# Computing the conditioning vectors of a decoder layer in couples: four column groups of TensorE, each with its own tile of outputs

## The reference

```
mod = (jax.nn.silu(c) @ w_ada + b_ada)[:, None, :]
shift_m, scale_m, gate_m, shift_f, scale_f, gate_f = jnp.split(mod, 6, axis=-1)
h = modulate(rms_norm(x, g_pre_mix), shift_m, scale_m)
... MIX(h): projection with w_in, pooling, dilated attention, merge, w_out ...
x = x + gate_m * rms_norm(mix, g_post_mix)
h = modulate(rms_norm(x, g_pre_ffn), shift_f, scale_f)
... FFN(h): w_up, depthwise convolution, GeGLU, w_down ...
x = x + gate_f * rms_norm(ffn, g_post_ffn)
```

## Time and profile before

| | |
|---|---|
| time, median of 3 runs | 1033.84 us (1033.68 to 1034.89) |
| span of the profiled execution, first to last instruction | 1030.3 us |
| TensorE (matmuls) busy | 98% of the span |
| TensorE weight loads busy | 94% |
| VectorE, ScalarE, GpSimd busy | 46%, 38%, 11% |
| mean granted TensorE clock | 0.996 of full |

### The profile page before, as it was taken

One profiled execution on the slowest core, in us unless ns is written; L12 is line 12 of the kernel. 1 busy time (PEld: TensorE's weight loads), 2 busy tenths in 40 slices (PEclk: granted clock), 3 DMA queues, 4 the chain that ended last, 5 costly groups with the idle time before them and its releaser, 6 DMA issues.

```text
span 1030.3 us, 20618 instructions
## 1 busy us (share of the span) xinstructions
PE 1010.5 (98%) x8733; PEld 973.6 (94%) x8733; DVE 472.8 (46%) x856; ACT 388.5 (38%) x633; POOL 112.8 (11%) x175
## 2 busy tenths in 40 slices
PE   7999999999999999999999998999999999999996
PEld 6899999999999999998989988999999999999996
DVE  6733324422433233325856447465656565532323
ACT  5334422433244224433113346445445444422232
POOL 1000300040004100334913000000000000000000
PEclk9999999999999999999999999999999999999998
DMA  9966476667665777539996682666666666566412
GB/s 325 304 223 205 151 250 236 236 195 251 238 242 178 240 251 263 173 93 354 374 310 192 226 257 66 199 208 230 216 225 221 224 223 198 192 211 198 122 47 83
DMA packets 226473, 222.32 MB, mean 216 GB/s; under 512 B 6301, under 2 KB 189981, under 8 KB 225597
## 3 DMA queue, kind: packets, MB, share of 16 engines
q1 hardware_dynamic: 226297, 220.85, 64.7%
q10 hardware_dynamic: 84, 0.15, 0.0%
HBM read 213.56 MB, written 96.03 MB: 300 GB/s over the span
## 4 chain that ended last, share of the span: by engine, by line
PE 90%; POOL 4%; DVE 2%; issue 1%; DMA 1%; ACT 1%; SPq 0%; ACTq 0%; DVEq 0%; POOLq 0%
PE acc L1501 74%; POOL cached L685 3%; PE acc L1592 2%; PE psT L1712 2%; PE psT L1725 1%; PE psS L1551 1%; PE psT L1739 1%; PE psS L1695 1%; PE acc L1607 1%; PE acc L1599 1%; POOL tha L692 1%; PE psT L1582 1%; DVE w_lo L993 1%; PE psS L1693 1%; PE psT L1623 1%
## 5 line engine op out<-in xcount | busy, mean ns | idle before, releaser
L1501 PE MATMUL acc<-act_hi,w_hi 128*128 128x260 f32 x1856 | 380.6, 286 | 1.4 <-DVE w_lo L993 0.8
L1501 PE MATMUL acc<-act_hi,w_lo 128*128 128x260 f32 x1856 | 373.7, 283 | 0.0
L1501 PE MATMUL acc<-act_lo,w_hi 128*128 128x260 f32 x1856 | 373.1, 283 | 0.0
L993 DVE TENSOR_TENSOR w_lo<-raw,w_hi 128x1024 fp32r<-128x1024 f32 (+1 forms) x148 | 185.1, 1252 | 324.4 <-ACT w_hi L711 324.0
L1501 PEld LDWEIGHTS acc<-act_hi,w_hi 128*128 128x128 f32 x1856 | 285.4, 188 | 10.1 <-issue 7.3
L1501 PEld LDWEIGHTS acc<-act_hi,w_lo 128*128 128x128 f32 x1856 | 285.8, 188 | 0.0
L1501 PEld LDWEIGHTS acc<-act_lo,w_hi 128*128 128x128 f32 x1856 | 285.5, 188 | 0.0
L711 ACT ACTIVATE w_hi<-raw 128x1024 fp32r<-128x1024 f32 (+1 forms) x148 | 154.7, 1047 | 138.9 <-PE acc L1501 130.0
L1501 PE MATMUL acc<-g_hi,w_hi 128*128 128x260 f32 x352 | 71.6, 285 | 0.0
L1501 PE MATMUL acc<-g_hi,w_lo 128*128 128x260 f32 x352 | 70.8, 282 | 0.0
L1501 PE MATMUL acc<-g_lo,w_hi 128*128 128x260 f32 x352 | 70.7, 282 | 0.0
(11 more groups left out here) (284 smaller groups left out, 1002.4 us busy)
## 6 DMA issues: line engine op xcount, KB each, us to landing
out_k_sample<-in_cache_k_w SPq DMA_DIRECT2D x89, 368.0 KB
out_v_sample<-in_cache_v_w SPq DMA_DIRECT2D x89, 368.0 KB
raw<-in_w_in SPq DMA_DIRECT2D x60, 512.0 KB, 9.2
raw<-in_w_up SPq DMA_DIRECT2D x44, 512.0 KB, 5.5
ada_last<-in_w_ada SPq DMA_DIRECT2D x12, 1024.0 KB, 9.5
ada_first<-in_w_ada SPq DMA_DIRECT2D x9, 1024.0 KB, 9.7
raw<-in_w_down SPq DMA_DIRECT2D x16, 512.0 KB, 4.3
out_k_sample<-in_cache_k_w SPq DMA_DIRECT2D x16, 511.0 KB
```

The lines of the kernel that those rows point to most:

```text
L993: dve.tensor_tensor(w_lo[PLACE[n]][:, 0:cols], raw[:, n % RAW, 0:cols], w_hi[PLACE[n]][:, 0:cols].bitcast(F32), ALU.subtract).then_inc(lo_ ...
L1501: ins_ = pe.matmul(acc[b][:, half, 0:HALF], w, x[:, t, half * HALF:(half + 1) * HALF], start=first and i == 0 and j == 0, stop=last and i ...
```

## The change

The 24 blocks become 12 couples of four output tiles (512 columns). ADA now lists couples as pairs (lo, hi) of the first tiles of two adjacent ones. A block s is now one half of a couple's contraction tiles: even s holds contraction tiles 0 to 3, odd s tiles 4 to 7, for all four output tiles. Every column group j owns output tile j of the couple and sums all eight contraction tiles. So ada(s) issues 16 matmuls of 128 x 128 in place of eight of 128 x 256. The sums of a couple are 128 x 128 in place of two times 128 x 256; one transpose (one load, one matmul) turns them, in place of four folding matmuls (eight loads, eight matmuls). The evacuation copies 128 columns per couple, one modulation serves a couple. The first eight loads are two DMAs of 512 KB each, with rows of 1 KB; later loads stay one DMA of 1024 KB, with rows of 2 KB. In the pairs stage the two blocks of a couple run one after the other in passes 1 and 3, with one fold each there; passes 0 and 2 have none. fold4 is gone.

```diff
-ADA = [0, 4, 1, 5, 2, 6, 3, 7] + list(range(8, 24))
+ADA = [(2 * j, 8 + 2 * j) for j in range(4)] + [(4 * c, 4 * c + 2) for c in range(4, 12)]
...
-                sp.dma_start(ada_slot(s)[:, :, :], block_of(w_ada, ADA[s] * 2 * P, 2 * P)).then_inc(ada_in[s % 8], 16)
+                lo, hi = ADA[s // 2]
+                src = tiles(w_ada)[:, s % 2 * 4:s % 2 * 4 + 4, :]
+                if s < SADA:
+                    for x, t in enumerate((lo, hi)):
+                        sp.dma_start(ada_slot(s)[:, :, 2 * P * x:2 * P * x + 2 * P], src[:, :, t * P:(t + 2) * P]).then_inc(ada_in[s % 8], 16)
+                else:
+                    sp.dma_start(ada_slot(s)[:, :, :], src[:, :, lo * P:(lo + 4) * P]).then_inc(ada_in[s % 8], 16)
...
-                act.wait_ge(folded, OADA + 2 * c)
-                act.activation(ada_rows[:, :, :, :].rearrange("p s a b -> p (s a b)"), psA_late[c], ACT.Copy).then_inc(ada_rowed, 2)
+                act.wait_ge(folded, MIDDLE + c - 1)
+                act.activation(ada_rows[:, c % 4, :], sums_of(MIDDLE + c), ACT.Copy).then_inc(ada_rowed, 1)
...
-                for k in range(KT):
-                    ins_ = pe.matmul(out[32 * (k % 4):32 * (k % 4) + 32, :], siluT[:, MC * k:MC * k + 32], ada_slot(s)[:, k, :], start=k < 4, stop=k >= 4)
+                for i in range(KT // 2):
+                    k = s % 2 * 4 + i
+                    for j in range(4):
+                        ins_ = pe.matmul(sums_of(c)[32 * j:32 * j + 32, :], siluT[:, MC * k:MC * k + 32], ada_slot(s)[:, i, j * P:(j + 1) * P],
+                                         start=k == 0, stop=k == KT - 1)
...
-                for i in range(2):
-                    ins_ = pe.matmul(out[:, i * MC:(i + 1) * MC], ada_rows[:, s % 2, i, :], fold4[:, :], start=True, stop=True)
-                ins_.then_inc(folded, 1)
+                pe.transpose(psM_first[c % 2] if c < FIRST else psM, ada_rows[:, c % 4, :], ident[:, :]).then_inc(folded, 1)
...
-                    elif what == "ada":
-                        ada(SADA + p * NA + k)
+                    elif what == "ada" and p % 2:
+                        ada(SADA + p - 1)
+                        ada(SADA + p)
...
-                for i in range(4):
-                    ins_ = pe.matmul(psM_late[c][:, i * MC:(i + 1) * MC], ada_rows[:, i // 2, i % 2, :], fold4[:, :], start=True, stop=True)
-                ins_.then_inc(folded, 2)
+                pe.transpose(psM_late[c], ada_rows[:, c % 4, :], ident[:, :]).then_inc(folded, 1)
```

More of the change, by code:

```diff
@@ L999, in of, with ada_evac, modulation @@
                 return accv[SUM[s] % 2]
[L1001 to L1011, removed]
+            def ada_evac(c):
+                dve.wait_ge(ada_done, 2 * c + 2)
+                if c >= 2:
+                    dve.wait_ge(folded, c - 1)
+                dve.tensor_copy(ada_rows[:, c % 4, :], sums_of(c)).then_inc(ada_rowed, 1)
+            def modulation(c):
+                dve.wait_ge(folded, c + 1)
+                lo, hi = ADA[c]
+                dst = mod[:, lo:lo + 2 * (hi - lo), :].rearrange("p (a b) m -> p a b m", a=2)[:, :, 0:2, :]
+                dve.tensor_tensor(dst, turned_of(c), four_tiles(vec, c).unsqueeze(3).to_broadcast([P, 2, 2, MC]), ALU.add).then_inc(ada_out, 1)
             def gains(dst, k0, nk, scale0, g0, plus):
@@ L1088, in _ @@
             dve.wait_ge(vec_out, 1)
-            for s in range(2):
-                ada_evac(s)
+            ada_evac(0)
             dve.wait_ge(rs_ready, 1)
@@ L1098, in _ @@
                 c = slice(2 * j, 2 * j + 2)
-                for s in (2 * j, 2 * j + 1):
-                    modulation(s)
-                dve.wait_ge(ada_out, 2 * j + 2)
+                modulation(j)
+                dve.wait_ge(ada_out, j + 1)
                 gains(a_m, 2 * j, 2, 8, 48, 1.0).then_inc(gained, 1)
@@ L1217, in _ @@
                         take_values(p, k)
-                    elif what == "ada":
-                        ada_evac(SADA + p * NA + k)
-                    elif what == "fold" and (p or k >= 0):
-                        modulation(SADA + p * NA + k)
+                    elif what == "ada" and p % 2:
+                        ada_evac(FIRST + p // 2)
+                    elif what == "fold" and p % 2:
+                        modulation(FIRST + p // 2)
                     elif what == "stat" and p:
@@ L1374, in _ @@
                 if m == 7:
-                    late_modulation(1)
+                    modulation(MIDDLE + 1)
                 take_samples(("out", m), m, gg_m)
@@ L1387, in _ @@
                     split(N["up", 0, 1])
-                    late_modulation(0)
+                    modulation(MIDDLE + 0)
             inverse_root(2)
@@ L1400, in _ @@
             dve.tensor_reduce(sSum[:, :], sSq[:, :, :].rearrange("p k b -> p b k"), AX_X, ALU.add).then_inc(xs_new_summed, 1)
-            late_modulation(2)
+            modulation(MIDDLE + 2)
             inverse_root(3)
@@ L1412, in _ @@
                 scaled(t, 0, 2)
-            late_modulation(3)
-            dve.wait_ge(ada_out, OADA + 8)
+            modulation(MIDDLE + 3)
+            dve.wait_ge(ada_out, MIDDLE + 4)
             gains(a_f, 0, KT, 32, 64, 1.0).then_inc(gained, 1)
@@ L1641, in _ @@
             fold(0)
-            fold(1)
             busy(30)
@@ L1658, in _ @@
                 first_units(2 * j - 2)
-                fold(2 * j)
-                fold(2 * j + 1)
+                fold(j)
                 first_units(2 * j - 1)
@@ L1793, in _ @@
                         values(p, k)
-                    elif what == "ada":
-                        ada(SADA + p * NA + k)
-                    elif what == "fold" and (p or k >= 0):
-                        fold(SADA + p * NA + k)
+                    elif what == "ada" and p % 2:
+                        ada(SADA + p - 1)
+                        ada(SADA + p)
+                    elif what == "fold" and p % 2:
+                        fold(FIRST + p // 2)
                     elif what == "stat" and p:
@@ L1912, in late_ada @@
             def late_ada(s):
-                c, at = (s - OADA) // 2, s % 2 * 2 * P
-                if c == 0:
+                c = (s - OADA) // 2
+                if s % 2 == 0 and c == 0:
                     pe.wait_ge(conv_used, 2)
-                if 2 <= c < LATE - 1:
-                    pe.wait_ge(ada_rowed, OADA + 2 * c - 2)
-                if c == LATE - 1:
+                if s % 2 == 0 and 2 <= c < LATE - 1:
+                    pe.wait_ge(ada_rowed, MIDDLE + c - 1)
+                if s % 2 == 0 and c == LATE - 1:
                     pe.wait_ge(rows_out, 8)
[L1921 to L1925, removed]
+                ada(s)
             def late_couple(c):
```

90 lines of the change are left out of this document (43 added, 47 removed).

## The result

The changed kernel takes 1025.97 us (median of 4 runs, 1025.8 to 1026.3), the kernel before 1034.37 beside it (1033.68 to 1034.93): ratio 0.9923, 95% interval 0.9909 to 0.9937. The nearest case was the rival to which I gave 0.2, that the feed doesn't bind (1026.9).

What follows compares the result with a forecast made beforehand. It took TensorE, busy 98% of the span, to bound the kernel. Terms -1.3 - 1.0 - 2.8 + 1.0 + 1.9 = -2.2 us, rounded to -2.1, took the median 1033.84 to 1031.8 us; range 1026.6 to 1037.5.

Steps and rivals of the forecast that it cites:

- the feed doesn't bind: Rival: 31 ns belongs to small turnings, not the sequencer, so bursts cost little more; -6.9, 1026.9 us, chance 0.2.
- the feed: On TensorE: the sequencer hands over an instruction every 31 ns, so two blocks in a row take 2.19 us against 1.86.
- a lead of instructions lying ready: Ahead of TensorE: instructions handed over early, at least 24 by one row, taken as 64, which shortens a burst's wait.
- Start stretch: Start of the kernel: cheaper folds and smaller copies against short leads and longer couples; net -1.2, with shorter modulation -1.3 us.
- the loads: Rival for the start: if split first loads land 1.3 us later, the start gains nothing; 1033.1 us, chance 0.1.
- Pairs stage: Pairs stage on TensorE: folds -1.4 us net of turnings, four single blocks becoming two bursts +0.4; net -1.0 us.
- Late folds: Late stage: folds 0, 1, 4 and 5 each become one turning of 0.11 us; together -2.8 us.
- Couples 0, 1 and 5: Late stage: three bursts of two blocks each take 0.33 us longer; together +1.0 us.
- Second norm: Second norm: doubled instructions end at 622.8 us, delaying the matmul that sums the samples and VectorE's norm; +1.9 us.
- the streaming rival: Rival that the columns streamed, not the handing over of instructions, set a burst; sum -6.9, 1026.9 us, chance 0.2.
- SyncE's wait for block 10: Fourth pass: SyncE waits some 6 us, hidden with 4 to spare; as a rival starving a unit, 1036 us, chance 0.05.
- What would show it: Test in the pairs stage: a burst of 2.1 to 2.3 us confirms feed and lead, 1.9 nothing binds, over 2.6 short lead.

Runs made afterwards that it cites:

- tiny_b: Changed kernel with 30 filler turnings ahead of block 2 replaced by three series with little to stream; one run, 1034.57 us, of no use as a time.
- two_loads: Changed kernel without the loads of blocks 2 to 7, which read two loaded slots again (output differs); 1025.48 us, ratio 0.9911.
- whole_loads: Changed kernel with its first eight loads whole (1 MB each) and both blocks of a couple run once both are there; 1028.04 us, ratio 0.9932.
- c0_after: The changed kernel again, no edit, as control beside the kernel before; 1025.96 us, ratio 0.9912.
- fold8: Changed kernel with each of the twelve folds issued as eight equal turnings; 1033.22 us, ratio 0.9993.
- c0_before: The kernel before again, unchanged, for a second profiled execution; 1034.79 us, ratio 1.0005.
- before_fill_b: The kernel before with useless filler turnings in the gaps of its second norm; 1032.74 us, ratio 0.9988.
- last_in_norm: Changed kernel with the last couple (blocks 22 and 23) moved from the up stage into gaps of the second norm; 1023.52 us, ratio 0.9893.
- halves: Changed kernel with every matmul of w_ada issued as two over 64 columns each; 1032.28 us, ratio 0.9976.
- group_order: Changed kernel with the 16 matmuls of a block issued one column group after another; 1050.02 us, ratio 1.0148.

## Why the prediction was wrong

The step that failed is **the feed**: "I read it as the rate at which TensorE's sequencer hands them over". The rate came from eight turnings with 128 weight columns, and I took for the instruction's price what was its weight load's. tiny_b varied that width (and the output's height with it) and the price fell from 64 to 27 ns a pair, the latter even at half the clock. And the burst that it was to price, 64 matmuls with their loads, took 1.88 us in place of the forecast's 2.19. The Trainium skill (TensorE: Matmul & The Clock Gate, section "LDWEIGHTS (loading the stationary operand)") says that a load's time follows the number of weight columns, not of rows. By that rule the row was a load's row, and the trace agrees (64 against 27 ns). I had cited the same page for about 62 ns per matmul, where firmware decodes them; here 64 matmuls of w_ada with their loads take 1.88 us, 29 ns each, and those of tiny_b's third series 15, so that price doesn't bind in this kernel. It looked confirmed because two different causes give nearly the same number.

My own row spoke against it: four blocks at 26 ns an instruction. I saved the theory with a lead of instructions lying ready, and then priced that lead at 64. The lead carried three of the four positive terms.

By the terms of the sum:

1. *Start stretch*, -1.3 forecast, -0.6 seen. The size was off for a reason that I had as a rival: the loads. The last landed at 38.50 (29.97 + 8.53) where before it was 36.5. By streaming the start was to gain 2.3; two_loads gains 2.5 (0.6 + 1.95). I had blamed the splitting; whole_loads shows that it is at most a small part. Of the 2 us between 0.7 and 1.7 stand already in the issue of the second group of first loads (14.86 us, and 14.29 in c0_after, against 13.15 and 13.61 in the two profiles of before). With whole loads it is 14.37, so the splitting doesn't make that part either; its cause stays open. TensorE's faster work then has nothing to run on. The 0.15 to 0.3 us that the forecast gave each of blocks 0, 1 and 3 for a short lead don't follow from its own rule, which gives 0.36 to 0.54 for leads of 27 and 21; no run shows such a term at all.
2. *Pairs stage*, -1.0 forecast, -2.5 seen. The bursts were to cost +0.4 and gave -0.5: a couple adds 0.9 us to a block's place and takes away a whole other block with its entry and exit, 1.15 by the starts of the units behind it. The folds gave -2.0, not -1.4: those that are left cost less on the chain than I took, since entering them is shorter too. No cover, as I had said.
3. *Late folds* -2.8, seen -2.7 (4 x 0.68 on the chain): right, and the largest single part; fold8 takes it back. *Couples 0, 1 and 5* +1.0, seen +0.06 (3 x 0.02).
4. *Second norm* +1.9, seen -0.25. The doubled instructions were done in time; L1973 waits for VectorE. The 10.35 us of supply for 334 instructions don't exist: from 609.30 to 617.30 some 390 ran in 8.0 us, 3.4 us of it at the lower clock.

The sum by the streaming rival was -6.9; seen in spans -6.2. The forecast also took the median as base, 1033.84, while its sum (-2.2, put down as -2.0) was made on a profile whose own time lay below it. Nothing told me that the kernel before loses some 2 us in most runs at a lower clock behind its second norm (c0_before, before_fill_b); that the changed kernel mostly escapes it is, by the mean clocks, the better part of the rest of the 8.4 us. Why it escapes is not shown. Fillers in the norm of the kernel before remove the stretch, but the changed kernel's own gaps (0.28, 1.45 and 1.40 us) don't guard against it: whole_loads, with nearly the same gaps, was caught in its profile, and so was two_loads, with longer ones.

*Costed at nothing*: the copies and modulations were hidden, as said. *SyncE's wait for block 10*: load_k(0) came at 366.30 in place of 363.46 (370 forecast) and no unit waited, as said. *What would show it*: "1.9 says that nothing binds" was the test that decided, at 1.88.

The range was too high by its lower end: 1026.6 took in the streaming rival with 0.3 us to spare, and nothing for the spread of the base.

## What to carry to other kernels

Before a rate read from small matmuls is taken for the sequencer's, look how wide their weight loads are, and look for one burst in the trace that runs faster; one is enough to refute it. With small weights split the work over TensorE's column groups in a round: it costs the same as fewer, longer matmuls (1.88 and 1.86 us a couple) and here saved the sums behind it, but in another order twice as much. Time won on TensorE is worth something only as far as the loads come along. An idle gap of TensorE is room for useful work: a couple moved into two of them gave back the 2.0 us that it had cost elsewhere (last_in_norm), and even useless work there spared the kernel before the lower clock behind it (1.35 us, before_fill_b). Before two kernels are compared by their medians, look at the granted clock of each run: by the mean clocks some 1.6 of the 8.4 us were of that kind.

## What the runs showed of the hardware

- w_ada's bursts ran at 7.5 ns per instruction (256 in 1.92 us, halves), but in that kernel TensorE stood four times without instructions: for 1.84 and 2.59 us within such bursts and for 1.24 and 0.88 us in units behind them. The profiles of the changed kernel, at 14.7 ns, have no wait of this kind in their lists.
- The granted clock fell to 0.5 for 3.4 us behind a stretch of one-column sums (610.2 to 613.6 us after, 614 to 617.6 in c0_before), though TensorE was busy throughout by the profile's count, and for 6.8 us behind a stretch in which it was busy 6.04 us of 6.70 (624.3 to 631.1 in c0_before). Neither is in every execution of the same kernel: the first profile of before has neither, with 4.75 us of 6.70 busy.
- Loading 128 weight columns for next to no moved ones took 64 ns a pair at a clock of 1.00; 8 weight columns took 27 and 32 columns in four groups 15, both at 0.50 (tiny_b). The Trainium skill (TensorE: Matmul & The Clock Gate, section "Back-to-back issue gap") gives some 25 ns as the issue floor of matmuls of 1 to 64 columns, or 62 with hardware decode off. The second series, 27, is near the floor; the third, 15, is under both.
- The order of issue: 64 matmuls of 32 weight columns and 128 moved ones took 1.88 us in a round over the four column groups and 4.26 us group by group, both at a clock of 1.00 (c0_after, group_order).
